# Behind the opening, two weight chunks per transfer of 1 MB into two neighbouring places of the ring

## The chip, the cores and the metric

The kernel runs on one core of a Trainium2 chip. The metric is the device time of one execution in microseconds, the median of several runs. The inputs lie in HBM; their layout is prepared on the host before the launch.

## What is computed

One layer of a decoder block for 256 tokens of width 2048 in float32: a SwiGLU feed-forward network (half step), a mix of dilated attention heads and retention heads, a second feed-forward network, and a last RMSNorm. Each part is preceded by an RMSNorm whose result is shifted and scaled, and followed by a gate; these nine vectors of 2048 come from a conditioning vector `c`.

```python
ada = (silu(c) @ w_ada + b_ada).reshape(b, 9, 1, 2048)   # sh1, sc1, gt1, sh2, ...
h = rmsnorm(x, g_ffn1) * (1 + sc1) + sh1
x = x + 0.5 * gt1 * ((silu(h @ w1_gate) * (h @ w1_up)) @ w1_down)
h = rmsnorm(x, g_mix) * (1 + sc2) + sh2
x = x + gt2 * token_mix(h, w_in, w_out)
h = rmsnorm(x, g_ffn2) * (1 + sc3) + sh3
x = x + 0.5 * gt3 * ((silu(h @ w2_gate) * (h @ w2_up)) @ w2_down)
out = rmsnorm(x, g_final)
```

The feed-forward width is 5632, the mix projects to 6144 columns. The weights, w_ada among them, are some 500 MB in all, and each is read once.

## The kernel before, in words

**Weights in chunks.** All weight matrices of the block are cut into 656 chunks (CHUNKS) in the order in which they are used. A chunk is two tiles of 128 rows by 512 columns, side by side: 128 partitions by 1024 float32 elements, 512 KB, 4 KB per partition. In HBM the chunks lie one behind the other (`w_all[c]`). A group of 8 to 12 chunks makes one result of 256 tokens by 512 columns in two PSUM banks.

**Split products.** To keep float32 accuracy, TensorE multiplies rounded high parts and remainders: high times high, high times low, low times high. For each chunk c, in order:
- SyncE's `w_chunk(c)` (L559 to L562) issues the load into place c % 4 of the ring `w_raw` (RING = 4), when the low part of chunk c - 4 is done (`lo_ready`), and the landing is counted on the semaphore `raw_in[c % 4]`.
- ScalarE's `w_hi(c)` (L647 to L653) waits for that landing and for TensorE to have finished the chunk whose place it takes in the ring `w_hi` (`w_free`; four places, and two more behind each normalisation), and casts `w_raw` to the high part.
- VectorE's `w_lo(c)` (L859 to L862) subtracts the high part from `w_raw` and writes the remainder to `w_lo`. This sets `lo_ready`, which both TensorE and SyncE's next load wait for.
- TensorE's `product_chunk(c)` (L1109 to L1123) makes 12 matmuls of 128 x 512 and counts `w_free`.

**The order on each engine** is written out in the program and is strictly in turn. In the loop behind the opening, ScalarE and VectorE go through the chunks: at step c ScalarE first casts chunk c + 4 and then does the stages that a table (SCHEDULE) puts at c; VectorE first does its stages at c and then the low part of chunk c + 4. Such stages are silu and product of a feed-forward group, turning the hidden layer, residuals, attention and retention, and the conditioning products.

**Conditioning.** w_ada is multiplied on VectorE: 144 tiles of 1 MB (8 KB per partition), each one product with a row-wise sum (`ada_tile`, L864 to L875). The first 32 are read in the opening through four places (`ada_early`). The other 112 go through two places (first `ada_raw_low`, then `ada_raw`) and are spread over chunks 51 to 469, in the first network one per 2 or 3 chunks. SyncE issues them with `late_tile` (L569 to L579): the first two behind the opening, when the modulated input is done (`mod_f32`), the others in the loop behind the weight load of the same number, 8 chunks behind the product that frees their place.

**The opening** (OPENING, L277 to L297) writes out the order of the first 50 chunks (OPEN_W = 50) and 32 tiles of w_ada, between which the first input is normalised, turned and modulated. The change leaves it as it is. Behind it stands SyncE's loop over chunks 50 to 655, which also holds the gate rows (stored and loaded again as a row, at steps 97 and 100, 217 and 272, and later), the rest of the constants' table (1664 KB, step 112) and the last gain row (step 596). Chunks 96 to 143 are the first down products, 264 to 359 the mix's input projections, 360 to 391 its output, 392 to 655 the second network.

Of the kernel before, what the change touches and what calls it, by code (L numbers as in the profile page):

```python
# [22 lines left out]
RING = 4  # L23
# [96 lines left out]
OPEN_W = OPEN_END - 4  # L120
# [31 lines left out]
def vector_done(v):  # L152

    return ADA_AT[max(i for i, m in enumerate(ADA_ORDER) if m // DT == v) - ADA_EARLY]
# [145 lines left out]
def ada_done(c):  # L300

    return ADA_EARLY + sum(at <= c for at in ADA_AT)
# [28 lines left out]
def build(nc, x_in, c_in, w_ada, b_ada, gains_in, g_final, w_all, table_in_hbm, out_t):  # L331
    with ExitStack() as ctx:  # L332
        def sb(name, shape, dt=F32):
            return ctx.enter_context(nc.sbuf_tensor(name, shape, dt))

        def sem(name):
            return ctx.enter_context(nc.semaphore(name))
# [11 lines left out]
        raw = sb("w_raw", [P, RING, CH])  # L349
# [57 lines left out]
        raw_in = [sem(f"raw_in{i}") for i in range(RING)]  # L407
# [4 lines left out]
        lo_ready = sem("lo_ready")  # L412
# [86 lines left out]
        def w_parts(c):  # L499

            at = SLOT[c]
            return (whi[:, at, :], wlo[:, at, :]) if at < RING else (whx[:, at - RING, :], wlx[:, at - RING, :])
# [21 lines left out]
        def last_before(n, u):  # L524

            quarter = QUARTERS.index((UNITS[u][0], UNITS[u][1] // 4)) - 2
            if quarter < 0:
                return SLICES + NU * (n - 1)
            return SLICES + NU * (n - 1) + max(i for i, (t, k, _) in enumerate(UNITS) if QUARTERS.index((t, k // 4)) == quarter) + 1
# [27 lines left out]
        @block.sync  # L557
        def _(sp):
            def w_chunk(c):  # L559
                if c >= RING:  # L560
                    sp.wait_ge(lo_ready, c - RING + 1)
                sp.dma_start(raw[:, c % RING, :], w_all[c]).then_inc(raw_in[c % RING], 16)  # L562

            def early_tile(i):
                if i >= EARLY:
                    sp.wait_ge(ada_step, i - EARLY + 1)
                sp.dma_start(ada_early[:, i % EARLY, :], w_ada[i]).then_inc(early_in[i % EARLY], 16)

            def late_tile(i):  # L569
                if i - ADA_EARLY >= LATE:  # L570
                    sp.wait_ge(ada_step, i - LATE + 1)
                else:
                    sp.wait_ge(mod_f32, SLICES)
                if i < ADA_EARLY + ADA_LOW:
                    place = ada_low
                else:
                    sp.wait_ge(restored, 4)
                    place = araw
                sp.dma_start(place[:, i % LATE, :], w_ada[i]).then_inc(ada_in[i % LATE], 16)  # L579

            def gate_store(layer):
                sp.wait_ge(gate_ready, layer + 1)
                sp.dma_start(gate_hbm[layer].rearrange("(p j) -> p j", j=DT), gate_col[:, :]).then_inc(gate_out, 16)

            def gate_load(layer):
                sp.wait_ge(gate_out, 16 * layer + 16)
                if layer == 0:
                    sp.wait_ge(restored, 6)
                else:
                    sp.wait_ge(res_free, (8, 12)[layer - 1])  # L590
                sp.dma_start(gate_row[:, :], gate_hbm[layer:layer + 1].to_broadcast([P, D])).then_inc(gate_in, 16)

            sp.dma_start(c_col[:, :], c_in).then_inc(c_in_sem, 16)
            sp.dma_start(tab[:, 0:EARLY_COLS], table_in_hbm[:, 0:EARLY_COLS]).then_inc(ident_in, 16)
            early_tile(0)
            sp.dma_start(ada[:, :], b_ada).then_inc(const_in, 16)
            sp.dma_start(gain[:, :, :], gains_in).then_inc(const_in, 16)
            early_tile(1)
            early_tile(2)
            for t in range(2):  # L600
                sp.dma_start(xs[:, t, :], x_in[:, t, :]).then_inc(x_in_sem[t], 16)
            early_tile(3)
            for kind, n in OPENING:
                if kind == "ada" and n >= EARLY:
                    early_tile(n)
                elif kind == "w":
                    w_chunk(n)

            late = {}
            for i in range(len(ADA_AT) - LATE):  # L610
                at = ADA_AT[i] + 8
                for n in (1, 2):
                    if ADA_AT[i] < NORM_AT[n] < ADA_AT[i + LATE]:
                        at = NORM_AT[n] + 12
                late.setdefault(at, []).append(ADA_EARLY + i + LATE)
            stores = {vector_done(v) + 8: layer for layer, v in enumerate(GATES)}
            loads = {max(vector_done(v) + 11, (0, MARKS["in"] + 8, MARKS["ffn2"] + 8)[layer]): layer
                     for layer, v in enumerate(GATES)}
            for i in range(LATE):
                late_tile(ADA_EARLY + i)  # L620
            for c in range(OPEN_W, CHUNKS):
                w_chunk(c)
                for i in late.get(c, ()):
                    if c - 12 in (NORM_AT[1], NORM_AT[2]):
                        sp.wait_ge(w_free, c - 12 + 3)
                    late_tile(i)
                if c in stores:
                    gate_store(stores[c])
                if c in loads:
                    gate_load(loads[c])  # L630
                if c == PARTED[-1].last + 17:
                    sp.wait_ge(restored, 8)
                    sp.dma_start(tab[:, EARLY_COLS:], table_in_hbm[:, EARLY_COLS:]).then_inc(table_in, 16)
                if c == CHUNKS - 60:
                    sp.wait_ge(ada_step, 9 * DT)
                    sp.dma_start(c_row[:, :], g_final.to_broadcast([P, D])).then_inc(final_in, 16)
            half = 2 * GW
            for t in range(2):
                sp.wait_ge(out_act, t + 1)
                sp.dma_start(out_t[:, t, 0:half], xs[:, t, 0:half]).then_inc(out_stored, 16)  # L640
                sp.wait_ge(out_dve, t + 1)
                sp.dma_start(out_t[:, t, half:], xs[:, t, half:]).then_inc(out_stored, 16)
            sp.wait_ge(out_stored, 64)

        @block.scalar
        def _(act):
            def w_hi(c):  # L647
                act.wait_ge(raw_in[c % RING], 16 * (c // RING + 1))
                if BEFORE[c] is not None:
                    act.wait_ge(w_free, BEFORE[c] + 1)  # L650
                if SLOT[c] >= RING:
                    act.wait_ge(ada_step, ada_done(c))
                nc.scalar.copy(w_parts(c)[0], raw[:, c % RING, :]).then_inc(hi_ready, 1)  # L653
# [89 lines left out]
            def modulate(m):  # L743
                n, u = m
                t, k0, tiles = UNITS[u]
                act.wait_ge(scl_ready, SLICES + n)
                act.wait_ge(xt_done, unit_count((n, max(i for i, (half, k, _) in enumerate(UNITS) if (half, k // 4) == (t, k0 // 4)))))
                act.wait_ge(mod_ready, last_before(n, u))
                for i in range(tiles):
                    k = k0 + i  # L750
                    ins = nc.scalar.activation(plain_unit(u)[:, i * P:i * P + P], turned(u)[:, i * P:i * P + P], ACT.Identity,  # L751
                                               scale=scl[:, k:k + 1], bias=ada[:, 3 * n * DT + k:3 * n * DT + k + 1])
                ins.then_inc(mod_f32, 1)
# [62 lines left out]
            keep_x(0)  # L816
            keep_x(1)
            w_hi(0)
            modulate_first(0)
            w_hi(1)  # L820
            normed_first(2)
            keep_x(2)
            keep_x(3)
            w_hi(2)
            normed_first(3)
            keep_x(4)
# [24 lines left out]
        def _(dve):  # L851
# [114 lines left out]
            def normed(m):  # L966
                n, (t, q) = m[0], QUARTERS[m[1]]
                if q >= 2:
                    last = max(u for u, (half, k, _) in enumerate(UNITS) if half == t and k // 4 == q - 2)
                    dve.wait_ge(xt_done, unit_count((n, last)))  # L970
                nc.vector.tensor_scalar(xn_buf(t, q), xs[:, t, GW * q:GW * q + GW], rinv[:, t:t + 1], None,  # L971
                                        ALU.mult).then_inc(xn_ready, 1)
# [447 lines left out]
```

## Time and profile before

| | us |
|---|---|
| time, median of 3 runs | 1901.14 |
| lowest, highest of them | 1900.92, 1901.29 |
| the profiled execution, its own time | 1900.6 |
| span of its core, first to last instruction | 1898.7 |
| mean granted TensorE clock | 0.998 |

| engine | busy us | share of the span |
|---|---|---|
| TensorE, matmuls | 1863.4 | 98% |
| TensorE, weight loads | 1542.2 | 81% |
| VectorE | 1306.0 | 69% |
| ScalarE | 859.3 | 45% |

Over the span 503.10 MB are read from HBM, 266 GB/s. The profile shows one execution. Its own time holds a little more than the span, since launch and end lie outside. In the tables of waits, an engine's idle time is put down to what ended it. A cast of `w_raw` that is released by "DMA" started when its chunk landed; one that is released by "PE banks" started when TensorE had left the place that it writes. The casts stand in order of the chunks, so counting them gives the chunk's number.

### The profile page before, as it was taken

The page shows a single profiled execution, that of the slowest core. Times are in us where ns is not written, and L with a number is a line of the kernel's source. Part 1 is how long each engine was busy: PE and PEld are TensorE (multiplying, and loading weights), DVE is VectorE, ACT ScalarE, POOL GpSimd, SP SyncE. Part 2 cuts the span into 40 slices and gives each one's busy share as a digit, 9 for nine tenths or more (in the row PEclk, how much of TensorE's full clock was granted, in tenths as well). Part 3 has the DMA queues.
Part 4 walks back from the last instruction along what each step waited for, and adds up shares of the span by engine and source line. Part 5 has one row for each costly group of instructions (what it writes and reads, how often), then busy time and mean ns, then how long its engine had stood idle before and what let it go on. Part 6 is the DMA issues. An engine that isn't in the chain of part 4 may idle for free. (4 is left out here: it accounts for less than half of the span.)

```text
span 1898.7 us, 21309 instructions
## 1 busy us (share of the span) xinstructions
PE 1863.4 (98%) x8392; PEld 1542.2 (81%) x8392; DVE 1306.0 (69%) x1355; ACT 859.3 (45%) x979; POOL 0.2 (0%) x4
## 2 busy tenths in 40 slices
PE   5999999999999999999999999999999999999998
PEld 4887888888888888788888887888888888888886
DVE  6997888888888888776655677666655554444464
ACT  6555544334444444645543546444443334444443
POOL 0000000000000000000000000000000000000000
PEclk9999999999999999999999999999999999999999
DMA  9998899999898998696454565777765656556564
GB/s 356 415 415 308 319 345 370 359 371 342 331 345 336 349 339 289 234 346 223 148 178 144 195 238 196 281 277 278 256 213 189 194 190 198 186 191 211 188 194 139
DMA packets 117890, 506.61 MB, mean 267 GB/s; under 512 B 13728, under 2 KB 13984, under 8 KB 98464
## 3 DMA queue, kind: packets, MB, share of 16 engines
q1 hardware_dynamic: 117792, 505.27, 73.1%
q8 instruction: 66, 1.08, 0.2%
q14 instruction: 32, 0.26, 0.0%
HBM read 503.10 MB, written 2.12 MB: 266 GB/s over the span
## 5 line engine op out<-in xcount | busy, mean ns | idle before, releaser
L862 DVE TENSOR_TENSOR w_lo<-w_raw,w_hi 128x1024 fp32r<-128x1024 f32 x652 | 794.6, 1223 | 500.0 <-ACT w_hi L653 498.9
L653 ACT CAST w_hi<-w_raw 128x1024 fp32r<-128x1024 f32 x652 | 684.5, 1051 | 967.0 <-PE banks L1120 904.4
L1118 PE MATMUL banks<-w_hi,x_split 128*128 128x512 f32 x1776 | 702.1, 395 | 6.4 <-DVE w_lo L862 4.1
L1120 PE MATMUL banks<-w_hi,x_split 128*128 128x512 f32 x1776 | 694.6, 391 | 0.0
L1119 PE MATMUL banks<-w_lo,x_split 128*128 128x512 f32 x1776 | 693.8, 391 | 0.0
L1118 PEld LDWEIGHTS banks<-w_hi,x_split 128*128 128x128 f32 x1776 | 334.7, 188 | 75.1 <-DVE w_lo L862 4.5
L1120 PEld LDWEIGHTS banks<-w_hi,x_split 128*128 128x128 f32 x1776 | 334.6, 188 | 70.5
L1119 PEld LDWEIGHTS banks<-w_lo,x_split 128*128 128x128 f32 x1776 | 334.8, 189 | 67.4
L1118 PE MATMUL banks<-w_hi,hidden 128*128 128x512 f32 x704 | 274.7, 390 | 0.0
L1120 PE MATMUL banks<-w_hi,hidden 128*128 128x512 f32 x704 | 274.3, 390 | 0.0
L1119 PE MATMUL banks<-w_lo,hidden 128*128 128x512 f32 x704 | 274.2, 390 | 0.0
L874 DVE CUSTOM_DVE_ANT_0 scratch<-ada_raw,cond_row,ada 128x2048 bf16<-128x2048 f32 x102 | 239.2, 2345 | 0.3
L1120 PEld LDWEIGHTS banks<-w_hi,hidden 128*128 128x128 f32 x704 | 132.2, 188 | 27.6
L1118 PEld LDWEIGHTS banks<-w_hi,hidden 128*128 128x128 f32 x704 | 132.2, 188 | 27.2
L1119 PEld LDWEIGHTS banks<-w_lo,hidden 128*128 128x128 f32 x704 | 132.2, 188 | 27.0
L874 DVE CUSTOM_DVE_ANT_0 scratch<-ada_early,cond_row,ada 128x2048 bf16<-128x2048 f32 x32 | 75.1, 2346 | 0.4
L1118 PE MATMUL banks<-w_hi,projections_split 128*128 128x512 f32 x128 | 50.2, 392 | 0.0
L1120 PE MATMUL banks<-w_hi,projections_split 128*128 128x512 f32 x128 | 49.9, 390 | 0.0
L1119 PE MATMUL banks<-w_lo,projections_split 128*128 128x512 f32 x128 | 49.9, 390 | 0.0
L895 DVE TENSOR_TENSOR scratch<-scratch,banks 128x1024 f32<-128x1024 f32 x22 | 26.8, 1219 | 4.5 <-PE banks L1120 4.3
L1120 PEld LDWEIGHTS banks<-w_hi,projections_split 128*128 128x128 f32 x128 | 24.0, 188 | 5.0
L751 ACT ACTIVATE scratch<-banks,ada,mod_scale 128x128 f32<-128x128 f32 x64 | 24.0, 468 | 9.2 <-issue 6.0
(132 smaller groups left out, 631.2 us busy)
## 6 DMA issues: line engine op xcount, KB each, us to landing
w_raw<-w_chunks SPq DMA_DIRECT2D x656, 512.0 KB, 4.3
ada_raw<-w_ada_tiles SPq DMA_DIRECT2D x102, 1024.0 KB, 6.7
ada_early<-w_ada_tiles SPq DMA_DIRECT2D x32, 1024.0 KB, 8.9
ada_raw_low<-w_ada_tiles SPq DMA_DIRECT2D x10, 1024.0 KB, 6.4
gate_row<-gate_rows SPq DMA_DIRECT2D x3, 1024.0 KB, 5.5
residual<-x_t SPq DMA_DIRECT2D x2, 1024.0 KB, 11.7
out_t<-residual SPq DMA_DIRECT2D x4, 512.0 KB, 3.1
table<-tables SPq DMA_DIRECT2D x1, 1664.0 KB, 9.6
```

The costliest lines, as they stand in the source:

```text
L653: nc.scalar.copy(w_parts(c)[0], raw[:, c % RING, :]).then_inc(hi_ready, 1)
L751: ins = nc.scalar.activation(plain_unit(u)[:, i * P:i * P + P], turned(u)[:, i * P:i * P + P], ACT.Identity, scale=scl[:, k:k + 1], bias=a ...
L862: nc.vector.tensor_tensor(lo, raw[:, c % RING, :], hi.bitcast(F32), ALU.subtract).then_inc(lo_ready, 1)
L874: nc.vector.tensor_tensor_reduce(junk, src, c_row[:, :], 1.0, ada[:, m:m + 1], ALU.mult, ALU.add, ada[:, m:m + 1]).then_inc(ada_step, 1)
L895: nc.vector.tensor_tensor(both(gate), both(gate), ps[:, 2 * g.side:2 * g.side + 2, :], ALU.mult).then_inc(hid_f32, 1)
L1118: nc.tensor.matmul(o, x_hi, hi, start=(first and k == k0), stop=False, skip_group_check=True)
L1119: nc.tensor.matmul(o, x_hi, lo, start=False, stop=False, skip_group_check=True)
L1120: ins = nc.tensor.matmul(o, x_lo, hi, start=False, stop=(last and k == k0 + KC - 1), skip_group_check=True)
```

## The change

Behind the opening a new function of SyncE, `w_pair`, loads chunks c and c + 1 (c even) in one transfer of 1 MB into the places c % 4 and c % 4 + 1 of `w_raw`. It waits until the low parts of both chunks that stood there are done, and its landing is counted on the semaphore of the even place. The cast of an odd chunk behind the opening waits on that semaphore too. At odd steps the loop issues no weight load; everything else in it stands where it stood.

```diff
@@ -561,6 +561,12 @@
                     sp.wait_ge(lo_ready, c - RING + 1)
                 sp.dma_start(raw[:, c % RING, :], w_all[c]).then_inc(raw_in[c % RING], 16)
 
+            def w_pair(c):
+
+                sp.wait_ge(lo_ready, c + 2 - RING)
+                sp.dma_start(raw[:, c % RING:c % RING + 2, :], w_all[c:c + 2].rearrange("c p n -> p c n")).then_inc(
+                    raw_in[c % RING], 16)
+
             def early_tile(i):
@@ -619,7 +625,8 @@
             for c in range(OPEN_W, CHUNKS):
-                w_chunk(c)
+                if c % 2 == 0:
+                    w_pair(c)
                 for i in late.get(c, ()):
@@ -645,7 +652,8 @@
             def w_hi(c):
-                act.wait_ge(raw_in[c % RING], 16 * (c // RING + 1))
+                landed = raw_in[c % RING if c < OPEN_W else c % RING // 2 * 2]
+                act.wait_ge(landed, 16 * (c // RING + 1))
                 if BEFORE[c] is not None:
```

## Rows read from the trace of the kernel before

**Rows 1.** The page, busy us of each engine, share of the span, instructions
```profile
PE 1863.4 (98%) x8392; PEld 1542.2 (81%) x8392; DVE 1306.0 (69%) x1355; ACT 859.3 (45%) x979; POOL 0.2 (0%) x4
```

**Rows 2.** Waits over the span: engine, line, released by: us in total, times, longest
```profile
ACT w_hi L653 <- PE banks L1120: 904.4, 563, 2.8
...
ACT w_hi L653 <- DMA w_raw<-w_chunks: 62.6, 40, 7.9
...
PE banks L1118 <- DVE w_lo L862: 4.1, 1, 4.1
```

**Rows 3.** Timeline of SyncE behind the opening: start us, us, instruction
```profile
161.33 0.80 SPq L579 DMA_DIRECT2D ada_raw_low<-w_ada_tiles  x2
162.18 21.95 SPq L562 DMA_DIRECT2D w_raw<-w_chunks  x10
```

**Rows 4.** Timeline of ScalarE, casts of chunks 50, 53, 54 [idle before, released by]
```profile
169.88 1.04 ACT L653 CAST w_hi<-w_raw 128x1024 fp32r<-128x1024 f32 x1 [7.92 <-DMA w_raw<-w_chunks]
...
173.71 1.04 ACT L653 CAST w_hi<-w_raw 128x1024 fp32r<-128x1024 f32 x1 [0.22 <-DMA w_raw<-w_chunks]
176.93 1.05 ACT L653 CAST w_hi<-w_raw 128x1024 fp32r<-128x1024 f32 x1 [2.18 <-PE banks L1120]
```

**Rows 5.** Timeline of TensorE, matmuls of chunk 50 and the first of 51
```profile
172.23 0.50 PE L1118 MATMUL banks<-w_hi,x_split 128*128 128x512 f32 x1 [4.07 <-DVE w_lo L862]
...
174.16 0.63 PE L1118 MATMUL banks<-w_hi,x_split 128*128 128x512 f32 x1
174.59 0.63 PE L1119 MATMUL banks<-w_lo,x_split 128*128 128x512 f32 x1
...
176.68 0.39 PE L1118 MATMUL banks<-w_hi,x_split 128*128 128x512 f32 x1
```

**Rows 6.** Windows: stretch, length, busy of PE, PEld, DVE, ACT, POOL, PEclk, DMA share, GB/s
```profile
173.00:176.60 3.60, 3.60 (x10) 2.81 (x9) 2.91 (x3) 1.54 (x2) 0.00 (x0) 0.53 0.90 241
...
180.00:750.00 570.00, 570.00 (x2561) 473.14 (x2560) 471.92 (x424) 248.95 (x251) 0.00 (x0) 1.00 0.90 342
```

**Rows 7.** Timelines of ScalarE and VectorE in an even stretch
```profile
208.69 1.05 ACT L653 CAST w_hi<-w_raw 128x1024 fp32r<-128x1024 f32 x1 [1.67 <-PE banks L1120]
211.41 1.05 ACT L653 CAST w_hi<-w_raw 128x1024 fp32r<-128x1024 f32 x1 [1.67 <-PE banks L1120]
...
208.20 2.35 DVE L874 CUSTOM_DVE_ANT_0 scratch<-ada_raw_low,cond_row,ada 128x2048 bf16<-128x2048 f32 x1
...
210.47 1.22 DVE L862 TENSOR_TENSOR w_lo<-w_raw,w_hi 128x1024 fp32r<-128x1024 f32 x1
212.50 1.23 DVE L862 TENSOR_TENSOR w_lo<-w_raw,w_hi 128x1024 fp32r<-128x1024 f32 x1 [0.80 <-ACT w_hi L653]
```

**Rows 8.** Landing by tile: w_raw (890 to 1050 us), ada_raw (all), ada_raw_low (160 to 240)
```profile
DMA to landing us min/median/max: 3.1/3.3/4.7
...
DMA to landing us min/median/max: 5.3/6.7/10.2
...
DMA to landing us min/median/max: 4.8/6.4/8.1
```

**Rows 9.** Timelines of SyncE (chunks 111, 112; 113, 114) and ScalarE (casts 113, 118)
```profile
329.19 3.74 SPq L562 DMA_DIRECT2D w_raw<-w_chunks  x2
...
334.35 3.73 SPq L562 DMA_DIRECT2D w_raw<-w_chunks  x2
...
344.37 1.05 ACT L653 CAST w_hi<-w_raw 128x1024 fp32r<-128x1024 f32 x1 [3.14 <-DMA w_raw<-w_chunks]
...
356.49 1.05 ACT L653 CAST w_hi<-w_raw 128x1024 fp32r<-128x1024 f32 x1 [1.67 <-PE banks L1120]
```

**Rows 10.** Timelines of SyncE (two tiles) and ScalarE (casts 276, 277, 279)
```profile
788.32 0.84 SPq L579 DMA_DIRECT2D ada_raw<-w_ada_tiles  x2
...
800.29 1.05 ACT L653 CAST w_hi<-w_raw 128x1024 fp32r<-128x1024 f32 x1 [4.16 <-DMA w_raw<-w_chunks]
801.56 1.06 ACT L653 CAST w_hi<-w_raw 128x1024 fp32r<-128x1024 f32 x1 [0.23 <-DMA w_raw<-w_chunks]
...
804.81 1.06 ACT L653 CAST w_hi<-w_raw 128x1024 fp32r<-128x1024 f32 x1 [0.95 <-PE banks L1120]
```

## The prediction

> **What bounds the kernel now.** I read the page first. TensorE is busy for 1863.4 of the 1898.7 us [rows 1]; the other engines and the DMA (mean 267 GB/s) have room over the whole. A change to weight loading can then act in one way only: it makes TensorE wait, or takes one of its waits away. So the second view was the table of waits [rows 2]. ScalarE's high casts (w_hi) mostly wait for TensorE (904.4 us in 563 waits), that is for a free place in the split ring, and rarely for a transfer (62.6 us in 40). TensorE itself waited once for a split weight behind the opening: 4.1 us.
>
> Third, the timelines around that wait. Behind the opening SyncE waits until the modulated input is done; at 161.33 it issues two 1 MB tiles of w_ada, and behind them chunks 50 to 53 from 162.18 on [rows 3]. Their four casts start as they land, the first at 169.88, after 7.92 us of waiting, the last at 173.71 [rows 4]: landings back to back, 1.28 us (3.83 over 3 gaps) per 512 KB. TensorE stood still for 4.07 us and began chunk 50 at 172.23 [rows 5]. Then its matmuls start 0.43 us apart [rows 5]; the windows give a granted clock of 0.53 from 173.0 to 176.6 and 1.00 from 180 to 750 [rows 6], so that is nearly all at the 1.2 GHz level, after an idle stretch. Chunk 50 takes until 176.68, 4.45 us, and a chunk at full clock 2.72 (below): the slow clock costs 1.7 us.
>
> Fourth, the even run. Casts start 2.72 us apart [rows 7]: one chunk. With PE the releaser, the cast of chunk c+4 starts about 0.24 us after TensorE leaves chunk c (chunk 54's at 176.93 [rows 4], TensorE on chunk 51 at 176.68 [rows 5]). So from the start of its own cast, a chunk is needed by TensorE 3 x 2.72 - 0.24 = 7.9 us later, and is ready after 1.05 + 0.04 + 1.22 = 2.3 us: **5.6 us in hand**, 4.9 where a w_ada product (2.35 us) sits before the low part [rows 7].
>
> **The change part by part.**
>
> *Issues.* From chunk 50 on, 606 weight issues become 303. Two tile issues take SyncE 0.80 us [rows 3]; at 0.4 us each some 120 us of SyncE go, in a queue that mostly waits for low parts: worth nothing.
>
> *The first half comes later.* Before, chunk c is issued when the low part of c-4 is done. A pair is issued when that of c-3 is done: 2.72 us later for the even chunk, unchanged for the odd one. Landing: a lone chunk takes 3.3 us (median of a quiet stretch [rows 8]), and the second 512 KB adds 1.28, so 4.6 us. Bounds: 3.3 (both halves as fast as one) and 6.7, the median of ada_raw's 1 MB transfers [rows 8], which however start right behind a weight chunk; even so their least is 5.3, and a w_ada tile with nothing ahead took 4.8 [rows 3, 8]. I take 4.6. Even run: cast c-3 + 2.34 to the end of its low part and the issue, + 4.6, against 3 x 2.72 = 8.16 to cast c: it lands 1.2 us early, 0.5 with a w_ada product in front. A late even half costs nothing for TensorE until the 5.6 us are gone, and the odd cast behind it is not moved until it is 1.67 us late (2.72 - 1.05).
>
> *Does lateness build up?* A slot pair goes round once per 4 chunks, 10.88 us. The round: landing + 1.05 (cast) + 2 x 1.22 (two low parts) + 0.1, and 2.35 for a w_ada product between the two, which is so for 2 of 5 pairs: landing + 4.5. With 4.6 this is 9.1, so late pairs catch up. It balances at a landing of 6.4 us.
>
> *w_ada tiles.* Their issue stands behind the weight issue of the same number. Of those issued in the loop, 52 stand at an even number and go 2.72 us later plus 1.28 of queue; the others only lose 1.28. Tile behind pair: 4.6 + 2.5 = 7.1 us after the pair's issue; + 2.35 + 1.22 = 10.7 until the odd low part behind its product, of 10.88 us. It fits, barely. The gate store and load, the constants' table (1.66 MB) and the last gain row keep their places in SyncE's order.
>
> *Chunk 50.* Nothing hides this one. Chunks 50 and 51 are one transfer now, whole when chunk 51 was: 1.28 us after chunk 50 was. Cast, low part and TensorE's start follow: **+1.3 us**. Bounds: 0 if the pair were there when chunk 50 was, +1.3 by the landings. The slow clock I leave at 1.7 us; bounds -0.2 and another +1.7, if the longer idle time doubles it.
>
> *Constants' table, chunks 112 to 115.* Table and one tile are issued between chunk 112 (the second issue of the row that ends at 332.93, so at 332.6) and chunk 113, at 334.35; cast 113 waits for its transfer until 344.37 [rows 9]. Now pair 112 goes at 334.35, then tile and table, then pair 114. Against chunk 113's landing that is 1.75 us later at the start and 2 x 1.28 more data up to its end: pair 114 lands near 348.6. Low part 114 is done at 348.6 + 2.3 = 350.9; the w_ada product that stands before low part 115 gets its tile 2.5 us behind the pair, at 351.1, so low part 115 is done at 351.1 + 2.35 + 1.22 = 354.7. TensorE wants 115 at 356.49 (cast 118 [rows 9]) - 0.24 = 356.25: 1.5 us left. I take 0, with 0 to 2 as bounds.
>
> *Start of the projections, chunk 276.* Here a gate row, issued in the loop's step 272, and two tiles (788.32) come close together. Cast 276 starts at 800.29 after a 4.16 us wait, so its low part is done at 802.6, and TensorE begins it at 804.81 (cast 279) - 0.24 = 804.57 [rows 10]: 2.0 us left. Chunk 276 now waits for chunk 277's data (cast at 801.56 [rows 10]: +1.28), and chunk 274's data has moved from before the queue into it: up to another 1.28. So 1.3 to 2.5 later, a wait of 0 to 0.6 us; with the gate row, now issued one chunk later too, holding up more, 1.2. I take +0.5.
>
> *Elsewhere* (attention's in-order ScalarE work behind a late cast, and boundaries): the weight landings there are quiet, 3.3 us [rows 8]; 0, bound 0.5.
>
> **Sum.** 1.3 + 0.5 = +1.8 us. On the profiled execution, 1900.6 us (span 1898.7 and 1.9 around it), that is 1902.4; the shown median is 1901.14, 0.5 above that execution, so 1902.9.
>
> *A rule against the trace.* The landings above lie 1.28 us apart, so two queued 512 KB transfers cost only their data [rows 4]. The Trainium skill ("DMA: Bandwidth & Descriptors", Anatomy of one DMA) gives each transfer about 2 us fixed beside bytes over 436 GB/s, and its Rules for kernel authors ask for 1 MiB or more per DMA. By that rule taken as a saving, an estimate from the page, chunk 50 would start 2.0 - 1.28 = 0.7 us sooner; the trace does not agree that queued transfers pay the fixed part in turn.
>
> **Rivals.** About 0.2% (3.8 us) is what a measurement of this kernel can tell from no change.
>
> *A: hidden at chunk 50 too* (the engines deliver the pair as one chunk, or its first half's work is absorbed): 1901.1. Against it: four landings evenly apart [rows 4].
>
> *B: the larger transfer pays off.* The mechanism is the queue: fewer transfers, shorter waits before chunk 50. At most the whole wait and its slow clock go: 4.07 + 1.7 = 5.8 us, 1895.3. Against it: 2 MB of w_ada data go ahead of the pair as before, and there is no other wait of TensorE for a split weight [rows 2]. The same 1 MiB rule of the Trainium skill's page "DMA: Bandwidth & Descriptors" (Rules for kernel authors) stands behind it.
>
> *C: thin places break.* The 1.5 us at chunk 115 and the 2.0 us at 276 fail together: waits of 2 and 1.2 us, one more slow-clock stretch of 1.7 us (one followed the 4.07 us of idle), with the 1.3: +6.2, so 1907.3. It decides if pair 114 lands past 351. For it: the DMA engines are 0.90 busy and VectorE 472 of 570 us over 180 to 750 [rows 6].
>
> *D: the ring's round becomes the bound*, on the slower side. Place: the w_ada stretch, chunks 58 to 256, about 50 rounds. If a pair lands after 6.7 us as ada_raw does [rows 8], the round is 11.25 us against 10.88, 0.37 x 50 = 18 us: 1919. It decides from 6.4 us. Against it: ada_raw's 6.7 contains the chunk ahead of it, and now a pair mostly finds an empty queue (pair and tile are 5.1 us of data per 5.44).
>
> **How the numbers follow.** Forecast 0.72 (own range 1901.5 to 1905.0), A 0.10, B 0.02, C 0.09, D 0.07. That no cast reads early is sure: odd chunks wait for the pair's semaphore. Faster by over 0.2%: B, 0.02. Slower by over 0.2%: C, D and 0.02 of the forecast's edge, 0.18. Within: 0.80. The range takes in A and leaves out B, C and D (0.18) and a little of the forecast's edges: 1901.0 to 1906.2.
>
> **What would show it.** Right: 353 weight issues; casts 50 and 51 back to back at about 171.2; TensorE's wait before chunk 50 at 5.3 us with one stretch near 0.5 clock; even casts in the w_ada stretch some times released by a transfer, waits for transfers up from 62.6 us to 150 or so, without TensorE waiting; pairs landing after 4.6 to 6 us; a wait under 1.2 us at chunk 276. Wrong: TensorE's waits for low parts in many places between 200 and 750 us, or a second slow-clock stretch (C, D); a wait before chunk 50 of 4 us or less (A, B).

## The result, and the profile after

| | us |
|---|---|
| changed kernel, median of 7 runs | 1907.29 |
| lowest, highest of them | 1905.56, 1911.99 |
| kernel before beside it, median of 7 runs | 1900.92 |
| ratio, 95% interval | 1.0040, 1.0028 to 1.0051 |
| profiled execution of the changed kernel, time and span | 1907.19, 1905.3 |

It is slower by 6.4 us between the medians and 7.6 us between the means, of which the ratio is made; +1.8 was forecast, and the time is outside the range of 1901.0 to 1906.2. It also spreads more: 6.4 us between its runs against 1.7 for the kernel before.

The page of the changed kernel (busy time by engine, as [rows 1]; the transfers of weights by size, count and us to landing) and its table of waits, whose first lines answer to [rows 2]:

```profile
PE 1864.9 (98%) x8392; PEld 1540.3 (81%) x8392; DVE 1305.8 (69%) x1355; ACT 853.3 (45%) x979; POOL 0.2 (0%) x4
...
w_raw<-w_chunks SPq DMA_DIRECT2D x303, 1024.0 KB, 4.9
...
w_raw<-w_chunks SPq DMA_DIRECT2D x50, 512.0 KB, 7.3
```

```profile
ACT w_hi L661 <- PE banks L1128: 601.2, 392, 2.8
DVE w_lo L870 <- ACT w_hi L661: 505.6, 372, 9.6
ACT w_hi L661 <- DMA w_raw<-w_chunks: 372.2, 141, 9.2
...
PE banks L1126 <- DVE w_lo L870: 7.7, 3, 5.5
```

The change is in place: 303 transfers of 1 MB. The work of each engine is the same. The casts now wait 372.2 us for transfers instead of 62.6, nearly all of it time that they waited for TensorE before (904.4 to 601.2 us). That alone costs nothing. But TensorE waits for a low part three times where it waited once.

**Chunk 50.** Timelines of SyncE, ScalarE and TensorE, and the windows (columns as in [rows 6]); they answer to [rows 3 to 6]:

```profile
160.56 0.80 SPq L585 DMA_DIRECT2D ada_raw_low<-w_ada_tiles  x2
161.41 15.31 SPq L567 DMA_DIRECT2D w_raw<-w_chunks  x4
```

```profile
170.40 1.99 ACT L661 CAST w_hi<-w_raw 128x1024 fp32r<-128x1024 f32 x2 [9.20 <-DMA w_raw<-w_chunks]
172.89 1.99 ACT L661 CAST w_hi<-w_raw 128x1024 fp32r<-128x1024 f32 x2 [0.50 <-DMA w_raw<-w_chunks]
```

```profile
172.75 0.80 PE L1126 MATMUL banks<-w_hi,x_split 128*128 128x512 f32 x1 [5.51 <-DVE w_lo L870]
...
175.48 0.63 PE L1126 MATMUL banks<-w_hi,x_split 128*128 128x512 f32 x1
175.91 0.63 PE L1127 MATMUL banks<-w_lo,x_split 128*128 128x512 f32 x1
```

```profile
171.60:178.50 6.90, 5.75 (x14) 4.50 (x15) 4.59 (x4) 2.78 (x3) 0.00 (x0) 0.51 0.58 212
178.50:182.00 3.50, 3.50 (x17) 2.89 (x16) 2.20 (x2) 3.25 (x3) 0.00 (x0) 1.00 0.62 254
```

Two pairs land, 2.49 us apart, and each releases two casts at once. TensorE stood still for 5.51 us (before 4.07), and the window shows the 1.2 GHz level over 6.9 us instead of 3.6; TensorE works in 5.75 of them. From its start on chunk 50 to its start on chunk 52 TensorE needs 8.24 us (to 180.99) where it needed 7.19 (172.23 to 179.42): 1.0 us more for the slow clock.

**The ends of groups ahead of a normalisation.** The other two waits of TensorE for a low part are these; the second is followed through the timelines of TensorE, ScalarE (casts 382, 384 and 385, 386 and 387, 388 and 389, 390 and 391) and VectorE (low part 386, residual, low parts 387, 388, 390):

```profile
760.67 0.50 PE L1126 MATMUL banks<-w_hi,hidden 128*128 128x512 f32 x1 [0.88 <-DVE w_lo L870]
...
1153.64 0.50 PE L1126 MATMUL banks<-w_hi,projections_split 128*128 128x512 f32 x1 [1.32 <-DVE w_lo L870]
```

```profile
1129.69 1.05 ACT L661 CAST w_hi<-w_raw 128x1024 fp32r<-128x1024 f32 x1 [3.35 <-DMA w_raw<-w_chunks]
...
1133.52 2.00 ACT L661 CAST w_hi<-w_raw 128x1024 fp32r<-128x1024 f32 x2 [0.32 <-DMA w_raw<-w_chunks]
1140.38 2.00 ACT L661 CAST w_hi<-w_raw 128x1024 fp32r<-128x1024 f32 x2 [4.86 <-DMA w_raw<-w_chunks]
...
1145.95 1.99 ACT L661 CAST w_hi<-w_raw 128x1024 fp32r<-128x1024 f32 x2
1151.27 1.99 ACT L661 CAST w_hi<-w_raw 128x1024 fp32r<-128x1024 f32 x2 [3.33 <-DMA w_raw<-w_chunks]
```

```profile
1141.47 1.22 DVE L870 TENSOR_TENSOR w_lo<-w_raw,w_hi 128x1024 fp32r<-128x1024 f32 x1 [3.79 <-ACT w_hi L661]
1142.61 1.28 DVE L919 TENSOR_TENSOR scratch<-banks,gate_row 128x512 f32<-128x512 f32 x2
1143.92 1.29 DVE L924 TENSOR_TENSOR residual<-residual,scratch 128x512 f32<-128x512 f32 x2
1145.13 1.22 DVE L870 TENSOR_TENSOR w_lo<-w_raw,w_hi 128x1024 fp32r<-128x1024 f32 x1
1147.02 1.23 DVE L870 TENSOR_TENSOR w_lo<-w_raw,w_hi 128x1024 fp32r<-128x1024 f32 x1 [0.67 <-ACT w_hi L661]
...
1152.35 1.23 DVE L870 TENSOR_TENSOR w_lo<-w_raw,w_hi 128x1024 fp32r<-128x1024 f32 x1 [2.71 <-ACT w_hi L661]
```

Read it backwards. (The low part of chunk 390 is called low part 390 here.) Low part 390 ends at 1153.58. Its pair was issued when low part 387 was done, at 1146.35, and was there 4.9 us later. Low part 387 stood behind a residual of 2.5 us on VectorE, whose engine had itself just waited 3.79 us for a late pair. In the kernel before, such a residual held up one load, that of the odd chunk; now it holds up both.

The lateness is older than these chunks. VectorE's low part 379 stands behind a w_ada product and a residual (low part 378, product, residual in two steps, low part 379):

```profile
1117.60 1.23 DVE L870 TENSOR_TENSOR w_lo<-w_raw,w_hi 128x1024 fp32r<-128x1024 f32 x1 [3.18 <-ACT w_hi L661]
1118.74 2.35 DVE L882 CUSTOM_DVE_ANT_0 scratch<-ada_raw,cond_row,ada 128x2048 bf16<-128x2048 f32 x1
...
1121.01 1.28 DVE L919 TENSOR_TENSOR scratch<-banks,gate_row 128x512 f32<-128x512 f32 x2
1122.33 1.30 DVE L924 TENSOR_TENSOR residual<-residual,scratch 128x512 f32<-128x512 f32 x2
1123.54 1.22 DVE L870 TENSOR_TENSOR w_lo<-w_raw,w_hi 128x1024 fp32r<-128x1024 f32 x1
```

From the issue of pair 378 (1111.70) to the end of low part 379 (1124.76), when pair 382 may go, this round takes 13.1 us; TensorE needs 10.88 us for four chunks. It is not the only such round, and the casts run late behind it: low part 388 is done 1.2 us ahead of TensorE's start on it (1148.25, 1149.43), where it was 5.0 us ahead before (1140.43, 1145.46).

And here TensorE asks for more. It takes the last four chunks of such a group in two passes, 128 tokens each, so that the next normalisation can begin with the first half. In the first pass a chunk lasts 1.36 us, not 2.72. From the start of the pass at 1149.43 the third chunk, 390, is wanted at 1152.15; it came 1.4 us too late. At 2.72 us per chunk it would have been wanted at 1154.87, and nothing had been lost. In the kernel before, the same chunk had 2.9 us left (VectorE's low part 390, TensorE's start on it):

```profile
1144.07 1.22 DVE L862 TENSOR_TENSOR w_lo<-w_raw,w_hi 128x1024 fp32r<-128x1024 f32 x1 [1.49 <-ACT w_hi L653]
...
1148.18 0.39 PE L1118 MATMUL banks<-w_hi,projections_split 128*128 128x512 f32 x1
```

The first half's end then comes late, and with it the residual and the transposes that open the normalisation. The residual starts 1.2 us behind the pass instead of 0.03, since the low parts of chunks 392 and 393, whose pair has landed only at 1154.49, stand before it on VectorE. So chunk 392 starts 6.56 us behind the kernel before where chunk 388 was 3.97 behind. That is 2.6 us in one place, of which 1.3 show as a wait for a weight. The third end of this kind, chunks 652 to 655, goes at the same pace and lost nothing: low part 654 was done 2.9 us ahead, as before. The pace costs only where the pairs are late already.

TensorE's start of each chunk, after less before, in the two profiled executions:

| chunk | later than before, us | what lies between |
|---|---|---|
| 49 | -0.9 | the opening, which the change leaves alone |
| 50 | +0.5 | +1.4: the pair's landing |
| 52 | +1.6 | +1.0: slow clock |
| 260 | +1.7 | 208 chunks without a loss |
| 264 | +3.2 | +1.4: first end ahead of a normalisation |
| 388 | +4.0 | +0.8: mostly chunks 326 and 379 |
| 392 | +6.6 | +2.6: second such end |
| 655 | +6.5 | nothing |

The -0.9 of the opening is no effect of the change: the profiles of the other kernels, with the same opening, stand between -1.4 and +0.2 at chunk 49. The losses behind it add up to 7.5 us.

### The profile page after: what moved, and what is told of

The parts are those of the page before. It is cut to its first block and busy times, and to the rows that moved or that the text cites. A ratio compares the mean times of both kernels' runs of the same rounds, so it can differ in the third digit from the quotient of the medians.

```text
span 1905.3 us, 21006 instructions
## 1 busy us (share of the span) xinstructions
PE 1864.9 (98%) x8392; PEld 1540.3 (81%) x8392; DVE 1305.8 (69%) x1355; ACT 853.3 (45%) x979; POOL 0.2 (0%) x4
## 5 line engine op out<-in xcount | busy, mean ns | idle before, releaser
L661 ACT CAST w_hi<-w_raw 128x1024 fp32r<-128x1024 f32 x652 | 678.4, 1050 | 974.0 <-PE banks L1128 601.2
L1126 PEld LDWEIGHTS banks<-w_hi,projections_split 128*128 128x128 f32 x128 | 24.0, 188 | 7.0 <-DVE w_lo L870 2.2
L1128 PEld LDWEIGHTS banks<-w_hi,projections_split 128*128 128x128 f32 x128 | 24.0, 188 | 5.1
```

The source lines that it names most:

```text
L1126: nc.tensor.matmul(o, x_hi, hi, start=(first and k == k0), stop=False, skip_group_check=True)
L1128: ins = nc.tensor.matmul(o, x_lo, hi, start=False, stop=(last and k == k0 + KC - 1), skip_group_check=True)
```

## The experiments

All times are medians beside runs of the kernel before on the same chip (1900.35 to 1900.61 us); the ratio is to those, with its 95% interval. Four runs take the loss apart by place.

**Chunks 50 and 51 single.** In the changed kernel, a set SINGLE of even chunks; a chunk in it and the one behind it go by `w_chunk`. Each cast waits for the count that the landings of its place have reached.

```diff
+SINGLE = {50}
-                if c % 2 == 0:
+                if c // 2 * 2 in SINGLE:
+                    w_chunk(c)
+                elif c % 2 == 0:
                     w_pair(c)
```

> Edit: as the changed kernel, but chunks 50 and 51 go in two transfers of 512 KB, each when its own place is free; pairs from 52 on. Theory P (three places): the loss of the change sits at chunk 50 (1.4 us by the later landing and 1.0 by a longer stretch at the 1.2 GHz level, read from the two traces) and at the two ends of groups ahead of a normalisation, chunks 258 to 263 and 386 to 391 (1.6 and 2.7 us). Then this run is about 2.5 us faster than the changed kernel, near 1904.8, TensorE's wait before chunk 50 is back at 4.1 us and the low clock lasts 3.4 us. Theory F (form): a 1 MB transfer in rows of two chunks is slower by itself, everywhere, and chunk 50 is not special: less than 0.7 us faster, near 1907.

Measured: 1904.96 us, ratio 1.0026 (1.0017 to 1.0035), 2.3 us less than the changed kernel. The wait ahead of chunk 50 is back at 4.1 us:

```profile
PE banks L1147 <- DVE w_lo L891: 5.3, 3, 4.1
```

Theory P holds for this place; theory F would have left the time as it was. The interval touches that of the changed kernel (1.0028 to 1.0051); the wait back at its old length is the stronger evidence.

**Chunks 256 to 263 and 384 to 391 single.**

```diff
+SINGLE = {*range(256, 264, 2), *range(384, 392, 2)}
```

> Edit: as the changed kernel, but chunks 256 to 263 and 384 to 391 go singly. Theory P: TensorE takes the last four chunks ahead of a normalisation twice, half a chunk of matmuls at a time, so it wants a new one every 1.36 us, and a late pair shows there. About 4 us faster than the changed kernel, near 1903, with chunk 260's and 388's halves free of waits of TensorE. If the lateness was gathered well ahead (VectorE behind the residuals, chunks 374 to 383), only half of it comes back: near 1905. Theory F: under 1 us faster, since only 16 of 606 chunks change their form.

Measured: 1903.80 us, ratio 1.0016 (1.0008 to 1.0025), 3.5 us less than the changed kernel. In the profile neither end of a group has a wait for a low part any more, and the first residual behind the first pass starts 0.03 us after it, as before. Sixteen chunks of 606 give back about half of the loss. Up to chunk 255 this kernel is the changed one, yet this execution lost 0.6 us at chunk 67, 1.8 at 114 and 0.9 at 115, 4.2 us in all between chunks 52 and 255, where the profile of the changed kernel lost 0.2: places that break in some executions and not in others. And chunk 50, a pair here too, cost less (TensorE's timeline, then windows as in [rows 6]):

```profile
173.72 0.79 PE L1147 MATMUL banks<-w_hi,x_split 128*128 128x512 f32 x1 [5.38 <-DVE w_lo L891]
...
173.20:176.70 3.50, 2.98 (x7) 2.40 (x8) 3.32 (x4) 2.15 (x3) 0.00 (x0) 0.51 0.14 23
176.70:180.00 3.30, 3.30 (x15) 2.68 (x15) 0.64 (x1) 0.38 (x1) 0.00 (x0) 1.00 1.03 418
```

TensorE was idle for 5.38 us, but the 1.2 GHz level lasted 3.5 us and not 6.9, and from chunk 50 to chunk 52 it took 6.96 us instead of 8.24.

**Both.**

```diff
+SINGLE = {*range(256, 264, 2), *range(384, 392, 2), 50}
```

> Edit: both of the above, chunks 50, 51, 256 to 263 and 384 to 391 singly, 293 pairs left. Theory P: the two gains add up, 6.5 us faster than the changed kernel, 1900.9 or up to 1 us above the kernel before (small waits at chunks 326 and 379 of 0.6 us stay). Theory F: 1905 or more.

Measured: 1902.24 us, ratio 1.0008 (0.9999 to 1.0017): 5.1 us less than the changed kernel, 1.6 above the kernel before. The two gains nearly add up; the forecast of 6.5 was too high.

**One pair alone, chunks 50 and 51.** All others single.

```diff
+SINGLE = {*range(52, CHUNKS, 2)}
```

> Edit: the kernel before with one single pair, chunks 50 and 51; all others go singly. It measures the term of the prediction that was 1.3 us, alone. Theory P (places): 1.3 us of later landing, and 0 or 1 us more if the low clock lasts two stretches of which TensorE is idle in a part: 1902 to 1903. Rival: the run with this pair alone made single won 2.3 us by chance of the opening, and this costs under 0.5: 1901.

Measured: 1901.93 us, ratio 1.0009 (1.0000 to 1.0018), +1.6 us for one pair, by the interval 0 to 3.4. In its profile:

```profile
172.39 0.80 PE L1147 MATMUL banks<-w_hi,x_split 128*128 128x512 f32 x1 [5.47 <-DVE w_lo L891]
```

The same 5.5 us of idle time as with all pairs, and the same long stretch of slow clock.

Next, what in a pair costs: the later issue, the common landing, or the form of the transfer.

**Two transfers at the pair's time, two semaphores.**

```diff
-                sp.dma_start(raw[:, c % RING:c % RING + 2, :], w_all[c:c + 2].rearrange("c p n -> p c n")).then_inc(
-                    raw_in[c % RING], 16)
+                for n in (c, c + 1):
+                    sp.dma_start(raw[:, n % RING, :], w_all[n]).then_inc(raw_in[n % RING], 16)
```

> Edit: the waits of the changed kernel stay (both chunks are issued when both places are free), but as two transfers of 512 KB with a semaphore each. It parts the late issue from the common landing. Theory P with the common landing as the larger part: chunk 50 gets its 2.5 us back, even chunks land 1.3 us sooner, the odd ones as before; at the ends of groups some of the 4.3 us stays, since the odd low part starts the next pair. 1903 to 1905. Theory F: as the kernel before, 1901, since the form is the old one. Theory L (late issue alone): as the changed kernel, 1906.5 to 1908.

Measured: 1901.94 us, ratio 1.0008 (0.9999 to 1.0016). Theory L falls: waiting for both places before the issue costs 1.3 us, at most 3 by the interval. The first of two lands sooner than a pair. In a quiet stretch (890 to 1050 us) the firsts take 3.2 us (median), and both are there 4.5 us after the first was issued; a pair takes 4.8. The views by tile give firsts and seconds together (this kernel's transfers of 512 KB, then the changed one's of 1 MB):

```profile
DMA to landing us min/median/max: 3.1/3.8/5.7
...
DMA to landing us min/median/max: 4.7/4.8/6.0
```

The time lies nearer to what theory F said, so one more run had to part the form from the common landing.

**The same two transfers, one semaphore.** Both casts wait for both transfers.

```diff
                 for n in (c, c + 1):
-                    sp.dma_start(raw[:, n % RING, :], w_all[n]).then_inc(raw_in[n % RING], 16)
+                    sp.dma_start(raw[:, n % RING, :], w_all[n]).then_inc(raw_in[c % RING], 16)
```

> Edit: as the run with two transfers of 512 KB issued together, but both count on one semaphore, and both casts wait for both, so the landing is common as in the changed kernel while the transfers have the old form. Theory C (common landing): the loss comes from the first chunk being usable only when the second has landed; as the changed kernel less at most 1 us, 1905.5 to 1907.5, with the second stretch of low clock back at chunk 50 or its 1.3 us. Theory F (form, the 1 MB transfer slower by itself: 4.85 us to land in quiet stretches against 4.54 for the second of two): as the two transfers with two semaphores, 1901.5 to 1903.

Measured: 1915.40 us (1909.77 to 1915.69), ratio 1.0069 (1.0057 to 1.0082). Transfers and the condition of their issue are those of the run before it; only what the casts wait for differs, and the time goes from 1901.94 to 1915.40 (means 1902.0 and 1913.7). So it is the common landing, and not the form; theory F falls. But theory C missed the size by 8 us. Waits of the two kernels (first with two semaphores, then with one):

```profile
ACT w_hi L660 <- DMA w_raw<-w_chunks: 207.5, 119, 8.0
```

```profile
ACT w_hi L665 <- DMA w_raw<-w_chunks: 431.3, 164, 9.3
```

Its profiled execution, the fastest of its runs, lost at chunks 57, 135, 148 and 162 too, in the stretch of the w_ada tiles, and at both ends of groups. Whether the other runs lost more at those places stays open, as does why it does worse than one transfer of 1 MB.

Last, a version without the wait at chunk 50, and the cost of pairs by stretch on top of it.

**The kernel before, reordered.** SyncE stood at the wait for the modulated input with four loads behind it that needed nothing of it.

```diff
-            for i in range(LATE):
-                late_tile(ADA_EARLY + i)
             for c in range(OPEN_W, CHUNKS):
+                if c == OPEN_W + RING:
+                    for i in range(LATE):
+                        late_tile(ADA_EARLY + i)
                 w_chunk(c)
```

> Edit: the kernel before, with the first two late tiles of w_ada issued behind chunk 53 instead of ahead of chunk 50, so SyncE does not stand at the wait for the modulated input with four free loads behind it. The wait of 4.07 us ahead of chunk 50 and its 1.7 us of low clock go: 5.8 us faster than the kernel before, 1894.8. Rival: the two tiles come too late for VectorE at step 51 and the wait moves there: 1898 or more.

Measured: 1894.52 us, ratio 0.9969 (0.9958 to 0.9981): 6.0 us faster than the kernel before, and faster than both kernels. SyncE's timeline (the load of chunk 53, then the two tiles) and ScalarE's casts of chunks 50 and 51, and 52, which do not wait for a transfer now:

```profile
160.76 0.33 SPq L562 DMA_DIRECT2D w_raw<-w_chunks  x1
161.13 0.91 SPq L579 DMA_DIRECT2D ada_raw_low<-w_ada_tiles  x2
```

```profile
161.34 2.00 ACT L654 CAST w_hi<-w_raw 128x1024 fp32r<-128x1024 f32 x2
164.92 1.05 ACT L654 CAST w_hi<-w_raw 128x1024 fp32r<-128x1024 f32 x1 [1.59 <-PE banks L1121]
```

The two tiles are issued when they were before (161.33 [rows 3]), and the loads of chunks 50 to 53 are ahead of them. The profile has no stretch at the 1.2 GHz level left between the opening and the end, and no wait of TensorE for a low part.

**The changed kernel with this order.**

> Edit: the changed kernel with the same reordering. Chunk 50 takes no part now, so what is left against the reordered kernel before is the cost of pairs elsewhere: as the run with chunks 50 and 51 single had (4.3 us above the kernel before), so 1899. If pairs lost only at chunk 50 and by chance elsewhere: 1895.

Measured: 1901.49 us, ratio 1.0007 (0.9998 to 1.0017), 7.0 us above the reordered kernel, where 4.3 was expected. Its profile lost 1.4 us at chunk 57 and 3.8 us more at chunks 123 to 162; at the second end of groups it lost 2.6 us as the changed kernel did, at the first 0.2 instead of 1.4. The wait at chunk 50 had also been time in which the ring filled up: low part 54 is done 2.7 us ahead of TensorE here, in the changed kernel 5.4. That fits the loss at chunk 57; that the later ones come from it too is not shown.

**With the ends of groups single as well.**

> Edit: the same, with chunks 256 to 263 and 384 to 391 single. Against the reordered kernel before it should keep the 1.6 us that the run with both sorts of single chunks kept against the kernel before: 1896.5. If the places at the ends of groups do not matter: as the run above, 1899.

Measured: 1898.54 us, ratio 0.9992 (0.9983 to 1.0000): 3.0 us less than the run above. The places at the ends matter here too, but 4.0 us stay elsewhere, where 1.6 was expected.

**Pairs in one stretch alone**, each on the reordered kernel before (1894.5). The kernel before stood at 1900.53 beside that one and at 1900.35 beside these three. The edits are the sets {50, *range(256, CHUNKS, 2)}, {*range(50, 264, 2), *range(392, CHUNKS, 2)} and {*range(50, 392, 2)} for SINGLE.

> Edit: the reordered kernel before (1894.5), with pairs for chunks 52 to 255 alone, the stretch of the w_ada tiles. In the profile of the reordered kernel with all pairs, TensorE lost 5 us here against the reordered kernel without (chunks 57, 115, 123, 135, 147, 162). Theory S (the slack is used up in the w_ada stretch and breaks at busy spots of VectorE and ScalarE): 3 to 5 us slower than the reordered kernel, 1897.5 to 1899.5. Theory B (only the ends of groups ahead of a normalisation break): under 1 us, 1895.5.

Measured: 1895.63 us, ratio 0.9976 (0.9966 to 0.9985): +1.1, at the bound that theory B gave and far from theory S. In its profile all of it is lost at chunk 57, and not to a weight: TensorE waits for the hidden layer's low part ahead of its transposes. The cast of chunk 54 waits 4.44 us for its pair, the first silu stands behind it on ScalarE, and by my reading product and split follow it late (timelines of ScalarE and TensorE):

```profile
172.91 1.05 ACT L683 CAST w_hi<-w_raw 128x1024 fp32r<-128x1024 f32 x1 [4.44 <-DMA w_raw<-w_chunks]
173.98 1.28 ACT L704 ACT_TABLE_LOAD   x1
175.27 1.03 ACT L704 ACTIVATE scratch<-banks 128x1024 f32<-128x1024 f32 x1
```

```profile
188.23 1.06 PE L1181 MATMUL banks<-table,scratch 128*128 128x128 f32 x8 [0.94 <-DVE hidden L930]
```

In the reordered kernel that silu starts at 172.88.

> Edit: the same, with pairs for chunks 264 to 391 alone: input projections, attention, retention and the output of the mix. Theory S and B alike: 0.5 us at chunk 326 and 2.5 to 3 us at 386 to 391, so 1897.5. If the lateness at chunk 386 comes from far ahead and not from the residuals just there, nothing changes, since it is all inside this stretch.

Measured: 1896.94 us, ratio 0.9982 (0.9973 to 0.9991): +2.4. Its profile has one wait of TensorE for a low part, at the third of the last four chunks:

```profile
PE banks L1148 <- DVE w_lo L892: 1.1, 1, 1.1
```

> Edit: the same, with pairs for chunks 392 to 655 alone, the second network with few or no w_ada tiles. Both theories: the pair lands 1 us before it is needed, the low parts keep 5.6 us, nothing is lost or won: 1894.5, within 0.3.

Measured: 1894.20 us, ratio 0.9967 (0.9955 to 0.9980): nothing. Of the 7.0 us that all pairs cost in this order, the stretches taken alone explain 3.5; chunks 50, 51 and 256 to 263, the first end among them, were in none of the three. The rest was not settled: in the profiles of the two kernels with pairs from chunk 50 on, 3.8 and 1.5 us are lost at chunks 123 to 162, where the run with pairs from 52 to 255 lost nothing. Up to there they differ in the pair 50, 51 alone, and one execution each was profiled.

What the traces do show is why these places are thin. At chunks 123, 135, 371 and 379 VectorE does a w_ada product and a residual before the low part, and in the kernel before it was done only 2.4 us ahead of TensorE, not 4.9. In the profile of the changed kernel 0.2 us were left at 123 and nothing at 135 and 379: a little more lateness, and TensorE waits.

## Why the prediction was wrong

- **Chunk 50** was right in place and mechanism. The term was +1.3; the two traces show +1.44 of idle time and +1.0 of slow clock. The slow clock was left at 1.7 us with +1.7 as a bound; it grew by 1.0 in this profile, and by nothing in that of the run with chunks 256 to 263 and 384 to 391 single. Measured alone the pair costs 1.6 us, measured by taking it away 2.3.
- **The step that failed is "Elsewhere": 0, bound 0.5.** It measured 4.8 us: 1.4 and 2.6 at the two ends, 0.8 between them. The 5.6 us in hand were worked out in an even run, where TensorE wants a chunk every 2.72 us. Ahead of a normalisation it wants one every 1.36 us, so the third of four chunks has 2 x 1.36 less: 2.9 us. The text had looked at landings (3.3 us, in a stretch that holds neither end: before the first one chunks 256 and 258 took 7.1 and 6.8 us) and not at TensorE's pace. 3.5 us came back when the two places were made single.
- **"A late even half costs nothing until the 5.6 us are gone"** held as far as it goes: 141 casts waited 372 us for transfers, over twice the 150 us expected, and over 200 chunks on end TensorE lost nothing. What it left out is that a residual on VectorE now holds up two loads.
- **"Late pairs catch up"** is the second half of that failed step. The round of 9.1 us, landing + 4.5, is a mean with the w_ada product in 2 of 5 rounds and no residual in any. Where both stand before the odd low part the round takes 13.1 us (pair 378) against 10.88, and lateness builds up; 4.9 us in hand were 2.4 there. How much of the 2.6 us at the second end is this lateness and how much TensorE's pace, no run parts.
- **Landing of a pair**: forecast 4.6, measured 4.8 in quiet stretches, 4.9 over all and 5.2 between 180 and 750 us (single ones up to 8.7); near enough. So rival D (6.7 us, balance at 6.4) did not happen.
- **Chunks 113 to 115 and 276**, on which the forecast spent 0.5 us and rival C its whole case, lost nothing in the profile of the changed kernel, though only 0.6 us were left at 115 where 1.5 were forecast. Chunks 114 and 115 did lose 2.7 us in one other execution. Rival C named almost the measured time, 1907.3, but by waits at other places than those of this profile: the number is luck; "thin places break" was right in it, and its longer slow clock came at chunk 50, not there.
- **Rivals A and B**: the pair was not there when chunk 50 was, and nothing got faster. The Trainium skill's advice of 1 MiB or more per transfer ("DMA: Bandwidth & Descriptors", Rules for kernel authors) brought nothing here; the saved issues were worth nothing, as said. The 2 us fixed per transfer that the prediction cites from that page (Anatomy of one DMA) are given there for transfers that GpSimd issues; here SyncE issues them.

The chance given to slower by more than 0.2% was 0.18, and that is what came.

## What to carry to other kernels

Merging two loads into one makes the first half wait for the second, and each load wait for the later of two places. Do it where the consumer has that much time in hand at its fastest pace, not at its mean pace: look for loops that are split in halves (the tails here; the heads, also taken in halves, lost nothing). And read the time in hand item by item, not as a mean: it was 5.6 us in the even run and 2.4 where product and residual fell on the same chunk. And look at what stands ahead of a load in the issuing queue: moving two issues behind four others that needed nothing of their wait gave 6 us here, more than any form of the transfer.

## What the hardware showed that was not expected

- At chunk 50, idle times of 4.1 to 4.2 us went with about 3.5 us at the 1.2 GHz level in four of four profiles; 5.4 to 5.5 us with about 6.9 in three and about 3.5 in one. So 1.4 us more of idle time cost 2.5 us in all in the changed kernel, and 1.3 us more cost 1.1 in that one profile. The length of the idle time alone does not say what a wait costs.
- Two transfers of 512 KB on two semaphores and one of 1 MB carry the same data at the same time of issue. In quiet stretches the 1 MB one landed after 4.8 us, the smaller ones after 3.8 (median over firsts and seconds), both of them 4.5 us after the first issue. Yet with one semaphore for both, the smaller ones made the slowest kernel of all, 1915.40 us. That the common landing costs this is shown; why more than in one transfer of 1 MB is not.
